# Second layer's gate and up projections: the two input halves side by side in one 512-column matmul

## The chip, the cores and the metric

One core of one Trainium2 chip runs the whole kernel. The metric is the device time of one execution in microseconds (us); the figure before is the median of three runs.

## The reference, cut to what matters

The model is one conformer-style block on 256 latent positions, followed by two layers of a diffusion-transformer block (D = 1024) on 256 latent and 256 context positions. The second of these layers needs no context output, so behind its attention it works on the 256 latent positions alone. Its feed-forward part is

```python
def swiglu(h, w_gate_up, w_down):
    gu = h @ w_gate_up
    g, u = jnp.split(gu, 2, axis=-1)
    return (jax.nn.silu(g) * u) @ w_down
```

with `w_gate_up` of 1024 x 5632 (gate and up, 2816 features each) and `w_down` of 2816 x 1024, all in float32.

## The kernel before, in words

**Precision.** TensorE multiplies in the type float32r, which keeps fewer bits than float32. So every weight W and every input x is held as a high part (the value rounded to float32r: `wh`, `xh`) and a low part (what is left: `wl`, `xl`), and a product is the sum of three matmuls, high by high, high weights by low input, and low weights by high input (`three`, lines 857 to 861). All three have 128 x 128 weights and a moving operand of 256 columns (one latent sequence, SEQ) or of 512 (latent and context, NT); in the second layer's feed-forward part it is 256.

**The weight stream.** All weights pass through SBUF in units of 128 x 1024 values (512 KB). There are four slots. For each unit SyncE loads `raw` (line 367) once GpSimd has made the low part of the unit four before it; ScalarE makes `wh` as a converting copy (line 548), once the unit has landed and TensorE is done with the unit four before it; GpSimd makes `wl = raw - wh` (line 475) and so releases the unit to TensorE. Each engine does its work in the order in which it is written, with semaphores between the engines.

**Gate and up of the second layer (phase `gu1`).** It has 22 steps. A step takes two units and gives one pair of output tiles, gate and up, of 128 features x 256 positions each: 2 outputs x 8 k-tiles x 3 matmuls = 48. I call the steps pairs 0 to 21. Steps alternate between two sets of PSUM banks (`j` = 0 and 1); before the change both tiles of a pair lie in one bank. When TensorE has finished a pair (`pair_done`), this happens: ScalarE applies Silu to the gate tile (line 699, into `sil`), VectorE multiplies it with the up tile (line 1358, `ft`), ScalarE makes its high part (line 702, `fh`), VectorE the low part (line 1361, `fl`).

**The order that matters.** In ScalarE's program (`gate_up` in the ScalarE block, lines 692 to 704), the body for pair p first converts the two units of pair p+1 (`high_step`), then waits for pair p, then does Silu and `fh`. So the units of pair p+2 are converted only behind `fh` of pair p, though their slots came free when TensorE finished pair p. GpSimd's two low parts for pair p+2 follow, and TensorE (`features`, from line 863) waits on each unit's low part before it starts it.

**Behind it** come the down projection `dn1` (12 steps of 48 matmuls, but each third one of 36, lines as above with `fh`, `fl` as input; ScalarE does nothing there but `high_step`) and a final norm and store.

Of the kernel before, what the change touches and what calls it, by code (L numbers as in the profile page):

```python
# [8 lines left out]
F32R = mybir.dt.float32r  # L9
BF16 = mybir.dt.bfloat16  # L10
ALU = mybir.AluOpType
ACT = mybir.ActivationFunctionType
AX_X = mybir.AxisListType.X

P = 128
D = 1024
KT = D // P
SEQ = 256
NT = 2 * SEQ
FF = 2816  # L20
FT = FF // P
# [38 lines left out]
PH, STEPS = plan()  # L60
# [19 lines left out]
XL_COUNT = {"m0": 6 * KT, "f0": 8 * KT, "m1": 10 * KT, "f1": 11 * KT}  # L80
# [18 lines left out]
ADA_SLOTS = 4  # L99
# [38 lines left out]
def build(nc, wall, wada, cond, xin, pin, par, tab, tab_ret, tab_rope, tab_mask, rpb, out):  # L138
    with ExitStack() as ctx:
        sems = {}  # L140

        def S(name):
            if name not in sems:
                sems[name] = ctx.enter_context(nc.semaphore(name))
            return sems[name]
# [8 lines left out]
        def at(name, shape, offset, dt=F32):  # L154
            size = 4 * int(np.prod(shape[1:]))
            assert offset + size <= base + arena_bytes, (name, offset + size - base - arena_bytes)
            return nc.alloc_sbuf_tensor_at(name, shape, dt, offset=offset)

        def sb(name, shape, dt=F32):
            o = cursor[0]  # L160
            cursor[0] = (o + 4 * int(np.prod(shape[1:])) + 31) // 32 * 32
            return at(name, shape, o, dt)
# [13 lines left out]

        h = sb("h", [P, KT, NT])
        xs_at = cursor[0]
        xh = sb("xh", [P, KT, NT], F32R)
        xl = sb("xl", [P, KT, NT], F32R)  # L180
        y = sb("y", [P, KT, NT])
        y_at = cursor[0] - 4 * KT * NT
        raw = sb("raw", [P, SLOTS, HALF, 256])
        wh = sb("wh", [P, SLOTS, HALF, 256], F32R)
        wl = sb("wl", [P, SLOTS, HALF, 256], F32R)
# [17 lines left out]
              NT: at("fl2", [P, FT, NT], big_at + 4 * FT * NT, F32R)}  # L203
        sil = at("sil", [P, 2, NT], y_at)
        ft = at("ft", [P, 2, NT], y_at + 8 * NT)


        r = Region(big_at, BIG)
# [50 lines left out]
        ps = ctx.enter_context(nc.psum_tensor("ps", [P, 8, 512], F32))  # L259
# [5 lines left out]
        ada_used = S("ada_used")  # L265
        bank_free = S("bank_free")
# [9 lines left out]
        def tile_bank(j, o, n, wide=False):  # L276

            return ps[:, j, o * SEQ:o * SEQ + SEQ] if n == SEQ and not wide else ps[:, 2 * j + o, 0:n]
# [25 lines left out]
        def pair_done(eng, ph, i, pair):  # L304

            eng.wait_ge(units_done, i * (2 * ph.body) + (2 * ph.step0 + 2 * ph.per_pair * (pair + 1) + SLOTS))
# [236 lines left out]
        def _(act):  # L543
# [145 lines left out]
            norm("fpre1", h, SEQ, 0)  # L689
            split("xr_ready", KT, y, SEQ, par_ap("ffn_pre"))  # L690

            def gate_up(ph, n, f0):

                def body(i):
                    for j in range(2):
                        high_step(ph, i, j)
                        pair_done(act, ph, i, j)
                        act.wait_ge(S("f_lo"), i * 2 + (f0 + j + 1))
                        nc.scalar.activation(sil[:, j, 0:n], tile_bank(j, 0, n), ACT.Silu).then_inc(S("silu_ready"), 1)  # L699
                        act.wait_ge(bank_free, i * 2 + (ph.pair0 + j + 3))  # L700
                        settled(act)
                        nc.scalar.activation(fh[n][:, i * 2 + j, :], ft[:, j, 0:n], ACT.Copy).then_inc(S("f_hi"), 1)  # L702
                preload(ACT.Silu)
                run(act, ph, body)
# [27 lines left out]
            for l in range(2):  # L732
# [102 lines left out]
                n = NT if l == 0 else SEQ  # L835
# [2 lines left out]
                split_shifted((3 + 2 * l) * KT, l, 3, n)  # L838
                if l == 0:
                    condition_to(csb_late)  # L840
                gate_up(PH[f"gu{l}"], n, FT * (l + 1))
                stream_only(PH[f"dn{l}"], peel=l)
            root("final", SEQ)

# [2 lines left out]
        def _(pe):  # L847
# [9 lines left out]
            def three(o, wa, wb, xa, xb, start, stop):  # L857

                nc.tensor.matmul(o, wa, xa, start=start, stop=False, skip_group_check=True)  # L859
                nc.tensor.matmul(o, wa, xb, start=False, stop=False, skip_group_check=True)  # L860
                return nc.tensor.matmul(o, wb, xa, start=False, stop=stop, skip_group_check=True)  # L861

            def features(ph, n, a=xh, b=xl, ktiles=KT, fresh=None, wide=False):


                def body(i):
                    for j in range(ph.body):
                        pair = j // ph.per_pair
                        if j % ph.per_pair == 0:
                            banks_ready(ph, i, pair)  # L870
                        for half in range(2):
                            slot = unit_ready(ph, i, j, half)
                            k0 = 2 * HALF * (j % ph.per_pair) + HALF * half
                            for o in range(2):
                                c = slice(o * P, o * P + P)
                                for kk in range(min(HALF, ktiles - k0)):
                                    k = k0 + kk
                                    if fresh and o == 0 and pair == 0:
                                        sem, n0, each = fresh
                                        pe.wait_ge(S(sem), n0 + each * (k + 1))  # L880
                                    mm = three(tile_bank(pair, o, n, wide), wh[:, slot, kk, c], wl[:, slot, kk, c],
                                               a[:, k, 0:n], b[:, k, 0:n], k == 0 and (n == NT or wide or o == 0), k == ktiles - 1)
                            mm.then_inc(units_done, 1)
                run(pe, ph, body)
# [53 lines left out]
            for hd in range(RET_H):  # L938
                b = hd % 2
# [13 lines left out]
            for hd in range(RET_H):  # L953
                pe.wait_ge(S("ret_s"), hd + 1)
                c = slice(hd * P, hd * P + P)
# [38 lines left out]
            for l in range(2):  # L994
# [158 lines left out]
                    pe.wait_ge(S("nol_ready"), 4)  # L1153
                features(PH[f"wo{l}"], n)
                norm_sum(f"f{l}", n)
                features(PH[f"gu{l}"], n, fresh=("xl_ready", XL_COUNT[f"f{l}"] - n // SEQ * KT, n // SEQ))
                features(PH[f"dn{l}"], n, fh[n], fl[n], FT, fresh=("f_lo", 2 + FT * (l + 1), 1))
            norm_sum("final", SEQ)

# [2 lines left out]
        def _(dve):  # L1162
            link = Link(dve, "dve_link")
            V = nc.vector

            for name, n in (("ada_used", ADA_SLOTS), ("bank_free", 2), ("f_lo", 2), ("osq_done", 2), ("npt_ready", 2), ("no_taken", 2)):
                dve.sem_inc(S(name), n)
            V.memset(up[:, :, 0:CONV_W - 1], 0.0)

# [56 lines left out]
            def condition(ph, i, j):  # L1226


                if ph.name not in ADA_WOVEN:
                    return  # L1230
                per, slots, a0, _ = ADA_WOVEN[ph.name]
                late = ph.name in ("gu0", "dn0")
                dve.wait_ge(S("cond_psum"), 6 if late else 2 if ph.name == "in_u" else 4)
                both = csb_late if late else csb_ps
                for s in range(per * j, per * j + per):
                    dve.wait_ge(ada_landed[s % slots],
                                i * (16 * 2 * per // slots) + 16 * (slot_tenants(ph.name, s % slots) + s // slots + 1))
                    at_ = bass.ds(i * (2 * per) + (a0 + s), 1)
                    dve.wait_ge(ada_used, i * (2 * per) + (a0 + s + ADA_SLOTS))
                    junk = unread[:].rearrange("p (a b) -> p a b", a=2)  # L1240
                    unit = ada_slot(ph.name, s % slots).rearrange("p (a b) -> p a b", a=2)
                    V.scalar_tensor_tensor(junk, unit, 1.0, both[0], ALU.mult, ALU.mult,  # L1242
                                           accum_out=mod_flat[:, at_, 0]).then_inc(S("ada_half"), 1)
                    dve.wait_ge(S("ada_half"), i * (2 * per) + (a0 + s + 1))
                    ins = V.scalar_tensor_tensor(junk, unit, 1.0, both[1], ALU.mult, ALU.mult,  # L1245
                                                 accum_out=mod_flat[:, at_, 1])
                    ins.then_inc(ada_used, 1)
# [101 lines left out]
                clear_sums(norm, n)  # L1349
                run(dve, ph, body)  # L1350

            def gate_up(ph, n, f0):
                def body(i):
                    for j in range(2):
                        condition(ph, i, j)
                        dve.wait_ge(S("f_lo"), i * 2 + (f0 + j + 1))
                        dve.wait_ge(S("silu_ready"), i * 2 + (f0 + j + 1))
                        V.tensor_tensor(ft[:, j, 0:n], sil[:, j, 0:n], tile_bank(j, 1, n), ALU.mult).then_inc(bank_free, 1)  # L1358
                        dve.wait_ge(S("f_hi"), i * 2 + (f0 + j + 1))
                        f1 = bass.ds(i * 2 + j, 1)  # L1360
                        V.tensor_tensor(fl[n][:, f1, :].rearrange("p a b -> p (a b)"), ft[:, j, 0:n],  # L1361
                                        fh[n][:, f1, :].rearrange("p a b -> p (a b)").bitcast(F32),
                                        ALU.subtract).then_inc(S("f_lo"), 1)
                run(dve, ph, body)
# [102 lines left out]
            for l in range(2):  # L1467
# [139 lines left out]
                take_gated(PH[f"wo{l}"], n, l, 0, f"f{l}")  # L1607
                recip(f"f{l}", n)
                modulate(l, 1, n)
                gate_up(PH[f"gu{l}"], n, FT * (l + 1))  # L1610
                if l == 0:
                    modulation(0, (5,))
                take_gated(PH[f"dn{l}"], n, l, 1, ("m1", "final")[l])
# [114 lines left out]
```

## Time and profile before

| | us |
|---|---|
| Median of 3 runs (1537.3 to 1539.34) | 1538.76 |
| The profiled execution's own time | 1542.9 |
| Its span, first to last instruction | 1540.8 |
| TensorE matmul busy | 1392.1 (90%) |
| GpSimd busy | 806.3 (52%) |
| VectorE busy | 819.4 (53%) |
| ScalarE busy | 590.9 (38%) |
| Gate and up of the second layer | about 1334 to 1464 of the span |
| Down of the second layer | about 1464 to 1528 |

The mean granted clock of TensorE is 0.947 of full speed. The profile is of one execution; its busy shares are averages over stages with different limits, and a matmul's busy time is longer than the distance between two matmuls, since they are pipelined. So the working below goes by start times in this stage.

### The profile page before, as it was taken

The page shows a single profiled execution, that of the slowest core. Times are in us where ns is not written, and L with a number is a line of the kernel's source. Part 1 is how long each engine was busy: PE and PEld are TensorE (multiplying, and loading weights), DVE is VectorE, ACT ScalarE, POOL GpSimd, SP SyncE. Part 2 cuts the span into 40 slices and gives each one's busy share as a digit, 9 for nine tenths or more (in the row PEclk, how much of TensorE's full clock was granted, in tenths as well). Part 3 has the DMA queues.
Part 4 walks back from the last instruction along what each step waited for, and adds up shares of the span by engine and source line. Part 5 has one row for each costly group of instructions (what it writes and reads, how often), then busy time and mean ns, then how long its engine had stood idle before and what let it go on. Part 6 is the DMA issues. An engine that isn't in the chain of part 4 may idle for free.

```text
span 1540.8 us, 25514 instructions
## 1 busy us (share of the span) xinstructions
PE 1392.1 (90%) x8734; PEld 1234.1 (80%) x8734; DVE 819.4 (53%) x1380; ACT 590.9 (38%) x938; POOL 806.3 (52%) x370
## 2 busy tenths in 40 slices
PE   5977899997789999696999999999699898799996
PEld 5976799996667878474788888888499877799996
DVE  5887755688843544736555556353504263711144
ACT  6434544444333434523332323222321264444442
POOL 3775488894535453140434444544174122588894
PEclk8998899998899999897999999999799998899998
DMA  7643377784322222010655554534094101355562
GB/s 278 228 131 137 123 273 274 277 308 144 116 67 71 83 69 83 14 55 28 224 184 191 190 215 169 203 137 177 25 258 116 41 2 54 109 179 179 187 205 95
DMA packets 82163, 227.16 MB, mean 147 GB/s; under 512 B 23872, under 2 KB 29248, under 8 KB 81856
## 3 DMA queue, kind: packets, MB, share of 16 engines
q1 hardware_dynamic: 81664, 224.91, 43.3%
q10 hardware_dynamic: 448, 1.57, 0.5%
q8 instruction: 31, 0.51, 0.1%
q14 instruction: 20, 0.16, 0.0%
HBM read 222.26 MB, written 1.05 MB: 145 GB/s over the span
## 4 chain that ended last, share of the span: by engine, by line
PE 43%; issue 33%; POOL 15%; DVE 6%; ACT 1%; DMA 1%; SPq 1%; POOLq 0%; DVEq 0%; ACTq 0%
POOL wl L475 14%; PE ps L859 11%; PE ps L860 11%; PE ps L861 11%; PE ps L902 1%; PE ps L901 1%; PE ps L900 1%; PE ps L1123 1%; PE ps L1137 1%; PE ps L1049 1%; PE ps L1075 1%; DVE rstd L1182 1%; PE ps L1115 1%; SPq L375 1%; DVE sq L1300 1%
## 5 line engine op out<-in xcount | busy, mean ns | idle before, releaser
L475 POOL TENSOR_TENSOR wl<-raw,wh 128x1024 fp32r<-128x1024 f32 x310 | 751.5, 2444 | 642.6 <-ACT wh L548 642.1
L859 PE MATMUL ps<-xh,wh 128*128 128x256 f32 (+1 forms) x1728 | 569.6, 330 | 53.5 <-DVE xl L1219 27.2
L860 PE MATMUL ps<-xl,wh 128*128 128x256 f32 (+1 forms) x1728 | 562.2, 325 | 0.0
L861 PE MATMUL ps<-xh,wl 128*128 128x256 f32 (+1 forms) x1728 | 561.8, 325 | 0.0
L548 ACT ACTIVATE wh<-raw 128x1024 fp32r<-128x1024 f32 x310 | 319.4, 1054 | 329.1 <-PE ps L861 211.1
L859 PEld LDWEIGHTS ps<-xh,wh 128*128 128x128 f32 x1728 | 336.2, 195 | 97.4 <-issue 55.5
L861 PEld LDWEIGHTS ps<-xh,wl 128*128 128x128 f32 x1728 | 336.7, 195 | 24.8
L860 PEld LDWEIGHTS ps<-xl,wh 128*128 128x128 f32 x1728 | 336.9, 195 | 23.2
L861 PE MATMUL ps<-fh,wl 128*128 128x256 f32 (+1 forms) x528 | 169.7, 321 | 0.0
L860 PE MATMUL ps<-fl,wh 128*128 128x256 f32 (+1 forms) x528 | 169.0, 320 | 0.0
L859 PE MATMUL ps<-fh,wh 128*128 128x256 f32 (+1 forms) x528 | 167.7, 318 | 0.0
L1358 DVE TENSOR_TENSOR ft<-sil,ps 128x256 f32<-128x256 f32 (+1 forms) x66 | 33.7, 510 | 193.1 <-ACT sil L699 193.1
L699 ACT ACTIVATE sil<-ps 128x256 f32<-128x256 f32 (+1 forms) x66 | 30.1, 456 | 222.9 <-PE ps L861 222.9
L859 PEld LDWEIGHTS ps<-fh,wh 128*128 128x128 f32 x528 | 100.0, 189 | 7.8
L860 PEld LDWEIGHTS ps<-fl,wh 128*128 128x128 f32 x528 | 98.9, 187 | 8.7
L861 PEld LDWEIGHTS ps<-fh,wl 128*128 128x128 f32 x528 | 99.1, 188 | 7.6
L1346 DVE SCALAR_TENSOR_TENSOR h<-ps,mod,h 128x256 f32 x48 | 20.3, 478 | 140.2 <-PE ps L861 140.0
L1242 DVE SCALAR_TENSOR_TENSOR unread<-ada_late,ps 128x1024 bf16<-128x1024 f32 x56 | 68.2, 1218 | 13.1 <-DMA ada_late<-wada 9.1
L1245 DVE SCALAR_TENSOR_TENSOR unread<-ada_late,ps 128x1024 bf16<-128x1024 f32 x56 | 68.4, 1221 | 8.2 <-DVE unread L1242 2.4
L1361 DVE TENSOR_TENSOR fl<-ft,fh 128x256 f32 (+1 forms) x66 | 36.2, 548 | 51.9 <-ACT fh L702 51.9
L756 ACT ACTIVATE e<-ps,sm 128x512 f32<-128x512 f32 (+1 forms) x64 | 36.4, 577 | 56.0 <-DVE sm L1493 39.9
L1242 DVE SCALAR_TENSOR_TENSOR unread<-ada,ps 128x1024 bf16<-128x1024 f32 x40 | 48.8, 1220 | 7.9 <-issue 3.9
(188 smaller groups left out, 1639.9 us busy)
## 6 DMA issues: line engine op xcount, KB each, us to landing
raw<-wall SPq DMA_DIRECT2D x310, 512.0 KB, 3.9
ada_late<-wada SPq DMA_DIRECT2D x56, 512.0 KB, 3.3
ada<-wada SPq DMA_DIRECT2D x40, 512.0 KB, 3.5
bias<-rpb SPq DMA_DIRECT2D x16, 256.0 KB, 7.7
h<-xin SPq DMA_DIRECT2D x2, 1024.0 KB, 7.1
sww<-qk SPq DMA_DIRECT2D x32, 64.0 KB, 2.0
csb<-cond SPq DMA_DIRECT2D x1, 1024.0 KB, 8.1
sw<-u ACTq DMA_DIRECT2D x2, 512.0 KB, 6.7
```

Source lines behind the costliest of these rows:

```text
L475: nc.gpsimd.tensor_tensor(wl[:, slot, :, :], raw[:, slot, :, :], wh[:, slot, :, :].bitcast(F32), ALU.subtract).then_inc(lo_ready, 1)
L548: nc.scalar.activation(wh[:, slot, :, :], raw[:, slot, :, :], ACT.Copy).then_inc(hi_ready, 1)
L699: nc.scalar.activation(sil[:, j, 0:n], tile_bank(j, 0, n), ACT.Silu).then_inc(S("silu_ready"), 1)
L756: nc.scalar.activation(e2[:, q, m, c], ps[:, b + m, c], ACT.Exp, scale=0.125, bias=sm[:, r6, 2 * t + m:2 * t + m + 1], accum_out=sm[:, r6, ...
L859: nc.tensor.matmul(o, wa, xa, start=start, stop=False, skip_group_check=True)
L860: nc.tensor.matmul(o, wa, xb, start=False, stop=False, skip_group_check=True)
L861: return nc.tensor.matmul(o, wb, xa, start=False, stop=stop, skip_group_check=True)
L1242: V.scalar_tensor_tensor(junk, unit, 1.0, both[0], ALU.mult, ALU.mult, accum_out=mod_flat[:, at_, 0]).then_inc(S("ada_half"), 1)
L1245: ins = V.scalar_tensor_tensor(junk, unit, 1.0, both[1], ALU.mult, ALU.mult, accum_out=mod_flat[:, at_, 1])
L1346: ins = V.scalar_tensor_tensor(hk, tile_bank(j, o, n)[:, t], g, hk, ALU.mult, ALU.add)
L1358: V.tensor_tensor(ft[:, j, 0:n], sil[:, j, 0:n], tile_bank(j, 1, n), ALU.mult).then_inc(bank_free, 1)
L1361: V.tensor_tensor(fl[n][:, f1, :].rearrange("p a b -> p (a b)"), ft[:, j, 0:n], fh[n][:, f1, :].rearrange("p a b -> p (a b)").bitcast(F32) ...
```

## The change

The high and the low input become two halves of one tensor `xhl` (same place, same order as before). In the second layer's gate and up, and there alone, the two matmuls that use the high weights become one with the moving operand `[high input | low input]`, 512 columns, into a whole PSUM bank; the third (low weights by high input) stays and adds to the bank's first half. Each pair so uses two banks in place of one. The second half of each bank must then be added to the first: ScalarE copies both second halves (128 x 512 values) to SBUF (`half_b`), VectorE adds them onto both first halves in PSUM, and Silu waits for that. In `features`, `joined` is used when `join` is given; `tile_bank(..., wide)` names the first half of the separate banks.

```diff
-        xh = sb("xh", [P, KT, NT], F32R)
-        xl = sb("xl", [P, KT, NT], F32R)
+        xhl = sb("xhl", [P, 2, KT, NT], F32R)
+        xh, xl = xhl[:, 0, :, :], xhl[:, 1, :, :]
...
+        half_b = at("half_b", [P, 2, SEQ], y_at + 16 * NT)
...
-            def gate_up(ph, n, f0):
+            def gate_up(ph, n, f0, join=False):
                 def body(i):
                     for j in range(2):
                         high_step(ph, i, j)
                         pair_done(act, ph, i, j)
+                        if join:
+                            act.wait_ge(S("halves_added"), i * 2 + (j + 1))
+                            nc.scalar.activation(half_b[:], ps[:, 2 * j:2 * j + 2, SEQ:NT], ACT.Copy).then_inc(S("half_copied"), 1)
+                            act.wait_ge(S("halves_added"), i * 2 + (j + 2))
                         act.wait_ge(S("f_lo"), i * 2 + (f0 + j + 1))
-                        nc.scalar.activation(sil[:, j, 0:n], tile_bank(j, 0, n), ACT.Silu).then_inc(S("silu_ready"), 1)
+                        nc.scalar.activation(sil[:, j, 0:n], tile_bank(j, 0, n, join), ACT.Silu).then_inc(S("silu_ready"), 1)
...
+            def joined(o, wa, wb, x, k, last):
+
+                nc.tensor.matmul(o, wa, x[:, :, k, 0:SEQ], start=k == 0, stop=False, skip_group_check=True)
+                return nc.tensor.matmul(o[:, 0:SEQ], wb, x[:, 0, k, 0:SEQ], start=False, stop=k == last, skip_group_check=True)
...
+                                    if join is not None:
+                                        mm = joined(ps[:, 2 * pair + o, :], wh[:, slot, kk, c], wl[:, slot, kk, c], join, k, ktiles - 1)
+                                        continue
...
-                features(PH[f"gu{l}"], n, fresh=("xl_ready", XL_COUNT[f"f{l}"] - n // SEQ * KT, n // SEQ))
+                features(PH[f"gu{l}"], n, fresh=("xl_ready", XL_COUNT[f"f{l}"] - n // SEQ * KT, n // SEQ),
+                         join=xhl if l else None)
...
-            def gate_up(ph, n, f0):
+            def gate_up(ph, n, f0, join=False):
                 def body(i):
                     for j in range(2):
                         condition(ph, i, j)
+                        if join:
+                            dve.wait_ge(S("half_copied"), i * 2 + (j + 1))
+                            two = ps[:, 2 * j:2 * j + 2, 0:SEQ]
+                            V.tensor_tensor(two, two, half_b[:], ALU.add).then_inc(S("halves_added"), 1)
...
-                        V.tensor_tensor(ft[:, j, 0:n], sil[:, j, 0:n], tile_bank(j, 1, n), ALU.mult).then_inc(bank_free, 1)
+                        V.tensor_tensor(ft[:, j, 0:n], sil[:, j, 0:n], tile_bank(j, 1, n, join), ALU.mult).then_inc(bank_free, 1)
```

## Rows read from the trace of the kernel before

**Rows 1.** The page's first part: busy time of each engine, share, instructions.
```profile
PE 1392.1 (90%) x8734; PEld 1234.1 (80%) x8734; DVE 819.4 (53%) x1380; ACT 590.9 (38%) x938; POOL 806.3 (52%) x370
```

**Rows 2.** Busy time by stretch: PE, PEld, DVE, ACT, POOL, clock, DMA share, GB/s.
```profile
1349.00:1464.00 115.00, 115.00 (x961) 115.00 (x960) 16.93 (x40) 55.07 (x80) 94.67 (x41) 1.00 0.55 183
...
1470.00:1520.00 50.00, 50.00 (x419) 50.00 (x419) 23.33 (x15) 21.49 (x21) 49.39 (x21) 1.00 0.57 189
```

**Rows 3.** Waits from 1344 to 1530: total us, times, longest.
```profile
POOL wl L475 <- ACT wh L548: 21.8, 22, 1.5
```

**Rows 4.** Timeline (start, us, instruction) of PE in the stage: 256 columns.
```profile
1383.06 0.28 PE L859 MATMUL ps<-xh,wh 128*128 128x256 f32 x1
1383.18 0.28 PE L860 MATMUL ps<-xl,wh 128*128 128x256 f32 x1
```

**Rows 5.** Timeline of PE in the first layer's gate and up: 512 columns.
```profile
899.79 0.39 PE L859 MATMUL ps<-xh,wh 128*128 128x512 f32 x1
...
903.87 0.39 PE L859 MATMUL ps<-xh,wh 128*128 128x512 f32 x1
```

**Rows 6.** Timeline of ACT over one pair of the stage.
```profile
1372.18 0.39 ACT L699 ACTIVATE sil<-ps 128x256 f32<-128x256 f32 x1 [2.40 <-PE ps L861]
1373.23 0.42 ACT L702 ACTIVATE fh<-ft 128x256 f32 x1 [0.67 <-DVE ft L1358]
1373.64 2.01 ACT L548 ACTIVATE wh<-raw 128x1024 fp32r<-128x1024 f32 x2
1377.95 0.38 ACT L699 ACTIVATE sil<-ps 128x256 f32<-128x256 f32 x1 [2.30 <-PE ps L861]
```

**Rows 7.** Timeline of DVE at the same pair.
```profile
1372.67 0.42 DVE L1358 TENSOR_TENSOR ft<-sil,ps 128x256 f32<-128x256 f32 x1 [4.20 <-ACT sil L699]
```

**Rows 8.** Timeline of POOL at this pair and the next.
```profile
1374.78 4.76 POOL L475 TENSOR_TENSOR wl<-raw,wh 128x1024 fp32r<-128x1024 f32 x2 [1.10 <-ACT wh L548]
1380.43 4.77 POOL L475 TENSOR_TENSOR wl<-raw,wh 128x1024 fp32r<-128x1024 f32 x2 [0.89 <-ACT wh L548]
```

**Rows 9.** Timeline of pairs 0 and 1, where PE once waits for POOL.
```profile
1340.56 4.76 POOL L475 TENSOR_TENSOR wl<-raw,wh 128x1024 fp32r<-128x1024 f32 x2 [16.87 <-ACT wh L548]
...
1341.91 0.28 PE L861 MATMUL ps<-xh,wl 128*128 128x256 f32 x1
1342.30 0.38 ACT L699 ACTIVATE sil<-ps 128x256 f32<-128x256 f32 x1 [0.87 <-PE ps L861]
...
1343.00 0.39 PE L859 MATMUL ps<-xh,wh 128*128 128x256 f32 x1 [0.81 <-POOL wl L475]
...
1348.86 0.28 PE L859 MATMUL ps<-xh,wh 128*128 128x256 f32 x1
...
1349.14 0.38 ACT L699 ACTIVATE sil<-ps 128x256 f32<-128x256 f32 x1 [3.48 <-PE ps L861]
```

**Rows 10.** Groups by line and shape: count, busy us, mean ns, idle before.
```profile
L767 ACT ACTIVATE pt<-ps 128x512 f32<-128x512 f32 x24 | 14.4, 598 | 41.3 <-PE ps L1064 41.3
...
L1580 DVE TENSOR_TENSOR ps<-ps,bias 128x512 f32<-128x512 f32 x16 | 11.2, 699 | 11.2 <-PE ps L1137 11.2
...
L1358 DVE TENSOR_TENSOR ft<-sil,ps 128x512 f32<-128x512 f32 x22 | 15.1, 688 | 69.4 <-ACT sil L699 69.4
```

**Rows 11.** Timeline: DVE operations that run beside POOL's low parts.
```profile
745.60 4.75 POOL L475 TENSOR_TENSOR wl<-raw,wh 128x1024 fp32r<-128x1024 f32 x2 [5.99 <-ACT wh L548]
...
749.81 0.69 DVE L1358 TENSOR_TENSOR ft<-sil,ps 128x512 f32<-128x512 f32 x1 [4.39 <-ACT sil L699]
...
1343.92 1.69 DVE L1361 TENSOR_TENSOR fl<-ft,fh 128x256 f32 x1 [0.71 <-ACT fh L702]
```

**Rows 12.** Busy time of PE alone in the attention stage: PE, clock, DMA, GB/s.
```profile
1285.00:1290.00 5.00, 3.91 (x34) 1.00 0.00 0
```

**Rows 13.** Timelines of ACT and POOL at the end of the stage (pair 21).
```profile
1464.34 0.38 ACT L699 ACTIVATE sil<-ps 128x256 f32<-128x256 f32 x1 [2.40 <-PE ps L861]
...
1466.84 44.21 POOL L475 TENSOR_TENSOR wl<-raw,wh 128x1024 fp32r<-128x1024 f32 x18 [1.01 <-ACT wh L548]
```

More of the change, by code:

```diff
@@ L840, in _ @@
                     condition_to(csb_late)
-                gate_up(PH[f"gu{l}"], n, FT * (l + 1))
+                gate_up(PH[f"gu{l}"], n, FT * (l + 1), l == 1)
                 stream_only(PH[f"dn{l}"], peel=l)
@@ L861, in three, with features @@
                 return nc.tensor.matmul(o, wb, xa, start=False, stop=stop, skip_group_check=True)
-            def features(ph, n, a=xh, b=xl, ktiles=KT, fresh=None, wide=False):
+            def joined(o, wa, wb, x, k, last):
+                nc.tensor.matmul(o, wa, x[:, :, k, 0:SEQ], start=k == 0, stop=False, skip_group_check=True)
+                return nc.tensor.matmul(o[:, 0:SEQ], wb, x[:, 0, k, 0:SEQ], start=False, stop=k == last, skip_group_check=True)
+            def features(ph, n, a=xh, b=xl, ktiles=KT, fresh=None, wide=False, join=None):
                 def body(i):
@@ L1164, in _ @@
             V = nc.vector
-            for name, n in (("ada_used", ADA_SLOTS), ("bank_free", 2), ("f_lo", 2), ("osq_done", 2), ("npt_ready", 2), ("no_taken", 2)):
+            for name, n in (("ada_used", ADA_SLOTS), ("bank_free", 2), ("f_lo", 2), ("osq_done", 2), ("npt_ready", 2), ("no_taken", 2), ("halves_added", 1)):
                 dve.sem_inc(S(name), n)
@@ L1609, in _ @@
                 modulate(l, 1, n)
-                gate_up(PH[f"gu{l}"], n, FT * (l + 1))
+                gate_up(PH[f"gu{l}"], n, FT * (l + 1), l == 1)
                 if l == 0:
```

## The prediction

> **What bounds the kernel now.** I began with the page: TensorE is busy 90% of the span, with one weight load for each matmul [rows 1]. That is an average, so I went to the stretches. From 1349 to 1464, gate and up of the second layer, TensorE is busy all the time at the full granted clock (1.00, the 2.4 GHz level), while GpSimd is busy 94.67 of 115 us; in the down projection behind it TensorE is full again, and GpSimd nearly so [rows 2]. The waits say the same: TensorE waits for nobody in this stage, and GpSimd waits 22 times for ScalarE, about 1 us each [rows 3]. So today the stage goes by the distance of matmuls, 0.12 us for 256 columns [rows 4], 48 x 0.12 = 5.76 us a pair. A shorter pair on TensorE would shorten the span one for one, as long as the next low part is there in time. How near that second limit is, the timelines of ScalarE, VectorE and GpSimd at one pair tell.
>
> **The second limit.** Take pair p, whose Silu starts at 1372.18 [rows 6]. VectorE's product starts at 1372.67 [rows 7], `fh` at 1373.23, and then ScalarE converts the two units of pair p+2, from 1373.64 [rows 6]. GpSimd starts on them at 1374.78, 2.60 us behind the start of Silu; for the other set of banks it is 1380.43 - 1377.95 = 2.48 [rows 6, 8]. One low part is 4.76 / 2 = 2.38, say 2.39. So the first low part of pair p+2 is done at 1377.17. TensorE wants it one pair behind pair p. Silu follows pair p's last matmul by 0.39 (1341.91 to 1342.30) [rows 9], and the next matmul would follow it by 0.12; so pair p+1 started at about 1372.18 - 0.39 + 0.12 = 1371.91, and p+2 starts at 1377.67. **The slack is 0.5 us**, or 0.6 in the other parity. The reader is to see that the chain runs over two pairs: end of pair p, Silu, product, `fh`, conversion, low part, pair p+2.
>
> One place shows TensorE at that limit: GpSimd's first low part of pair 1 ends at 1340.56 + 2.38 = 1342.94, and TensorE starts the pair at 1343.00, 0.06 later, after a wait of 0.81; Silu of that pair comes at 1349.14, and pair 2 would start at 1348.86, which is 5.86 after the start, so a stalled start costs 0.10 more than a flowing one [rows 9].
>
> **What the change removes.** 22 pairs x 2 outputs x 8 k-tiles = 352 matmuls and as many weight loads go. The columns stay: 768 per k-tile. 512 columns take (903.87 - 899.79) / 18 = 0.227 us [rows 5], where two of 256 take 0.240 [rows 4]; 0.0133 x 352 = 4.7 us. A pair becomes 16 x (0.227 + 0.120) = 5.55 us, 0.21 less. By the Trainium skill (TensorE: Matmul & The Clock Gate, Back-to-back issue gap) an isolated warm matmul needs N / 2.4 + 2.5 ns, which as an estimate would make a removed matmul worth 2.5 ns, 0.9 us for all 352. The rows differ, with 13.3 ns over the columns' time, and the rows decide.
>
> The moving operand now consists of two runs of 256 columns in two places. No row shows such a one. It can hardly be faster than one run; slower by at most what splitting it costs today, 0.0133 a matmul, 0.21 a pair. I take nothing, as the 512-column rows are the nearest, and keep 0.21 for the range.
>
> **What it adds**, for each pair, all of it ahead of Silu, and so in the chain of two pairs:
> - ScalarE's copy of 128 x 512 out of PSUM: 0.60 (line 767, 24 of them, mean 598 ns) [rows 10].
> - ScalarE to VectorE: Silu ends at 1372.57, the product starts at 1372.67: 0.10 [rows 6, 7].
> - VectorE's add of 128 x 512 in place in PSUM: 0.70. Line 1580 is the same form, two half banks and an SBUF operand, mean 699 ns [rows 10].
> - VectorE to ScalarE: the product ends at 1373.09, `fh` starts at 1373.23: 0.14 [rows 6, 7].
>
> Together X = 1.54 us. It can't be below 0.60 + 0.69 = 1.29, the two operations alone; above, three more register-addressed waits a pair could each show a little: I allow 0.3 and take 1.54.
>
> The price of the add needs a look, since GpSimd is at work beside it. `fl` of pair 0 (both inputs in SBUF) took 1.69 in place of 0.42 while a low part ran; the product with one input in PSUM took 0.69, undisturbed, beside low parts that run from 745.60 to 750.35 [rows 11]. The add has one input in each, so it goes by the second. The Trainium skill (SBUF — State Buffer, SBUF: two separate sides) says that a VectorE operation with two SBUF inputs and a GpSimd operation that reads SBUF exclude each other; by that rule, the trace agrees, 1.69 against 0.69.
>
> What waits behind the new wait: on ScalarE the Silu, `fh` and both conversions for pair p+2; then GpSimd, TensorE, and SyncE's loads, which go by GpSimd's low parts. Banks, `sil` and `half_b` are free in time: the product frees the banks under 3 us behind the pair's end, and they are wanted 5.5 us behind it. The weights' loads have time too: a slot is reloaded from the end of its low part and converted some 8.9 us later. The new first waits of copy (`halves_added`) are met already. Moving `xh` and `xl` into one tensor changes no address and costs nothing.
>
> **The sum.** From a stalled start of an odd pair to the start two pairs later: 0.10 + 5.55 of TensorE, less one distance of 0.12 and plus 0.39 to the copy: 5.92; X 1.54; Silu to GpSimd 2.60; low part 2.39; release 0.06. **12.51 us for two pairs**, against 11.52 now and 11.10 if TensorE set the pace. For the even pairs it is 12.39. So the slower, odd chain sets it: from pair 1 (1343.00, whose start hangs on a conversion that ScalarE does at 1339.44, ahead of anything new) over pairs 3, 5, ... 21 to the second step of the down projection, whose units are converted behind pair 21's `fh` just the same: 11 double steps, 137.6 us, to 1480.6. Today that step starts 21 x 5.76 = 120.96 after pair 2's 1348.86, at 1469.8. **The change costs 10.8 us**; the removed 4.7 are in it.
>
> Behind that the down projection stays as it is. TensorE takes 2.88 a unit, GpSimd 44.21 / 18 = 2.46 [rows 13], so GpSimd runs ahead again; only each sixth unit takes TensorE 1.44, where its lead shrinks to some 0.3. I take nothing, and keep 1 us for the range. Silu of the last pair should come at 1343.00 + 10 x 12.51 + 5.92 + 1.54 = 1475.6 in place of 1464.34 [rows 13].
>
> The profiled execution took 1542.9, 4.1 above the median of 1538.76. 1542.9 + 10.8 = 1553.7 for such a one; the median should be 1538.8 + 10.8 = 1549.6, or 0.7% more.
>
> **The rivals.**
> - *Faster: TensorE still sets the pace.* The place is the wait for the low part of pair p+2. If the chain's slack covered X, the whole 4.7 us would come: 1534.0. Without X and without a stalled start the odd chain takes 12.51 - 1.54 - 0.10 = 10.87 us, against 11.10 of TensorE; so X must stay under 11.10 - 10.87 = 0.23 for the full gain, and under 11.52 - 10.97 = 0.55 for any. The copy alone is 0.60. For it speaks that TensorE never waits today; against it all of rows 6 to 10. Chance 0.03.
> - *No change within 0.2%*: X from about 0.3 to 0.8 (0.55, and 3.1 / 11 = 0.28 to either side), if copy and add overlapped or the two handshakes vanished. They can't overlap, each waits for the other. Chance 0.03.
> - *The clock.* A TensorE that stalls each second pair by 1 us could be granted 1.2 GHz at times. Where it was busy for 3.91 of 5 us it kept 1.00 [rows 12], and here it would be busy 89%. Were one pair in ten at the lower level, that is two pairs, 11 us more: 1561. Chance 0.03.
> - *The add is held up by GpSimd* as `fl` was: X grows by about 1.0 in most pairs, 11 us more: 1561. Chance 0.04, since the rows of 11 speak against it.
> - *The new operand is slow* (0.21 a pair, once per double step, 2.3 us) and the waits show (0.3 x 11 = 3.3 us): that is still the forecast's case, up to 1556.
>
> **How the numbers follow.** The chain as reckoned has 0.87. Its own range: X from 1.29 to 1.84 is -2.8 to +3.3 us, the operand up to +2.3, the down projection up to +1, not all at once; with the even chain setting the pace 1.3 less. That gives 1545 to 1556, and as the other cases hold 0.13 the range stays there. A difference of about 0.2%, 3 us, is what a measurement of this kernel can tell from none. Faster 0.03, same 0.03, slower 0.94.
>
> **What would show it.** In the changed trace TensorE waits for GpSimd's `wl` in the stage, about 1.0 us ahead of odd pairs and 0.3 or less ahead of even ones, where there was no wait; GpSimd's idle time before it, put down to ScalarE's `wh`, grows from 1 to about 1.5 us a pair; Silu starts come 12.5 us apart over two pairs; copy 0.60, add 0.70, copy to Silu 1.54; distances of 0.227 and 0.12 on TensorE; clock 1.00. Pairs of 5.55 without waits would prove me wrong, and so would an add of over 1 us or a copy-to-Silu distance under 0.6.

## The result and the profile after

The changed kernel takes 1546.65 us (median of 7 runs, 1543.08 to 1551.38), the kernel before 1537.3 (7 runs, 1534.23 to 1541.2): ratio 1.0061, interval 1.004 to 1.0081. It is slower by some 9 us, where 10.8 were forecast.

The page of the changed kernel, where span and TensorE's row answer to [rows 1]:

```profile
span 1541.3 us, 24921 instructions
PE 1388.5 (90%) x8382; PEld 1210.8 (79%) x8382; DVE 844.8 (55%) x1402; ACT 604.4 (39%) x960; POOL 805.7 (52%) x370
```

The span is only 0.5 us above that of before, and that misleads. This profiled execution took 1543.08, the lowest of its seven, and that of before 1542.9, above all seven of its own; the stages ahead of the change ran 8.4 us shorter in it (the stage's first matmul starts at 1325.64 in place of 1334.06). They are the same work in both. So I compare **from the stage's first matmul to the end of the span**: 1540.8 - 1334.06 = 206.7 us before, 1541.3 - 1325.64 = 215.7 after, 8.9 more. The experiments are read with the same two points.

Timelines of the changed kernel at pairs 1 to 3, merged from TensorE, ScalarE, VectorE and GpSimd (start us, us, instruction); they answer to [rows 6 to 9]:

```profile
1334.59 0.49 PE L870 MATMUL ps<-xhl,wh 128*128 128x512 f32 x1 [0.75 <-POOL wl L476]
1334.93 0.28 PE L871 MATMUL ps<-xhl,wl 128*128 128x256 f32 x1
...
1340.13 0.28 PE L871 MATMUL ps<-xhl,wl 128*128 128x256 f32 x1
1340.45 0.60 ACT L701 ACTIVATE half_b<-ps 128x512 f32<-128x512 f32 x1 [1.69 <-PE ps L871]
1341.08 0.70 DVE L1373 TENSOR_TENSOR ps<-ps,half_b 128x512 f32<-128x512 f32 x1 [3.63 <-ACT half_b L701]
1341.89 0.38 ACT L704 ACTIVATE sil<-ps 128x256 f32<-128x256 f32 x1 [0.84 <-DVE ps L1373]
1342.37 0.42 DVE L1376 TENSOR_TENSOR ft<-sil,ps 128x256 f32<-128x256 f32 x1 [0.60 <-ACT sil L704]
1342.92 0.42 ACT L707 ACTIVATE fh<-ft 128x256 f32 x1 [0.65 <-DVE ft L1376]
1343.34 2.01 ACT L549 ACTIVATE wh<-raw 128x1024 fp32r<-128x1024 f32 x2
1344.47 4.74 POOL L476 TENSOR_TENSOR wl<-raw,wh 128x1024 fp32r<-128x1024 f32 x2 [1.82 <-ACT wh L549]
...
1345.89 0.27 PE L871 MATMUL ps<-xhl,wl 128*128 128x256 f32 x1
1346.91 0.50 PE L870 MATMUL ps<-xhl,wh 128*128 128x512 f32 x1 [0.75 <-POOL wl L476]
1347.26 0.28 PE L871 MATMUL ps<-xhl,wl 128*128 128x256 f32 x1
...
1352.55 0.28 PE L871 MATMUL ps<-xhl,wl 128*128 128x256 f32 x1
```

The reader is to follow one turn of the chain. Pair 1 starts at 1334.59; its end reaches ScalarE at 1340.45; copy, add and their handshakes put Silu at 1341.89; the conversions for pair 3 come at 1343.34, GpSimd at 1344.47, and pair 3 starts at 1346.91, where TensorE, done with pair 2, would have started at about 1346.0. 12.32 us for two pairs. TensorE waits like this ahead of every odd pair and ahead of the second step of the down projection, 12 times in all: 0.53 to 0.93 us each by the waits' rows, the first of them (0.75) being the one that before had too. Ahead of even pairs the rows list none; the most that the starts show is 0.13, at pair 6. The last two lines, of pair 3, are for the experiments on the matmuls.

The waits of the changed kernel from 1330 to 1535, total us, times, longest; the first row answers to [rows 3]:

```profile
POOL wl L476 <- ACT wh L549: 48.5, 24, 16.9
...
PE ps L870 <- POOL wl L476: 9.0, 11, 0.9
```

Less the one wait of 16.9 ahead of the stage, GpSimd now waits 31.6 us for ScalarE, 23 times, 1.4 each. A stretch of the stage, with [rows 2] for comparison (columns as there):

```profile
1349.00:1460.00 111.00, 103.51 (x575) 87.41 (x574) 27.82 (x54) 60.07 (x90) 85.08 (x37) 1.00 0.50 168
```

TensorE, busy throughout before, is busy 93% now, at the full granted clock, and GpSimd 77%: neither is the bound. The bound is the chain through all four engines.

### The profile page after: what moved, and what is told of

Read it like the earlier page. It is cut to its first block, busy times and chain, and to the rows that moved or that the text cites. A ratio compares the mean times of both kernels' runs of the same rounds, so it can differ in the third digit from the quotient of the medians.

```text
span 1541.3 us, 24921 instructions
## 1 busy us (share of the span) xinstructions
PE 1388.5 (90%) x8382; PEld 1210.8 (79%) x8382; DVE 844.8 (55%) x1402; ACT 604.4 (39%) x960; POOL 805.7 (52%) x370
## 4 chain that ended last, share of the span: by engine, by line
PE 60%; issue 19%; POOL 12%; DVE 5%; SPq 1%; ACT 1%; DMA 0%; POOLq 0%; DVEq 0%; ACTq 0%
PE ps L864 17%; PE ps L866 16%; PE ps L865 16%; POOL wl L476 11%; PE ps L915 1%; PE ps L914 1%; PE ps L913 1%; PE ps L1136 1%; PE ps L1088 1%; PE ps L1062 1%; PE ps L1150 1%; DVE rstd L1196 1%; PE ps L1128 1%; DVE y L1225 1%; SPq L376 1%
## 5 line engine op out<-in xcount | busy, mean ns | idle before, releaser
L864 PE MATMUL ps<-xhl,wh 128*128 128x256 f32 (+1 forms) x1376 | 466.6, 339 | 49.0 <-DVE xhl L1233 23.0
L865 PE MATMUL ps<-xhl,wh 128*128 128x256 f32 (+1 forms) x1376 | 459.8, 334 | 0.0
L866 PE MATMUL ps<-xhl,wl 128*128 128x256 f32 (+1 forms) x1376 | 459.7, 334 | 0.0
L864 PEld LDWEIGHTS ps<-xhl,wh 128*128 128x128 f32 x1376 | 266.3, 194 | 91.6 <-issue 48.0
L866 PEld LDWEIGHTS ps<-xhl,wl 128*128 128x128 f32 x1376 | 266.8, 194 | 24.5
L865 PEld LDWEIGHTS ps<-xhl,wh 128*128 128x128 f32 x1376 | 267.1, 194 | 22.9
L870 PE MATMUL ps<-xhl,wh 128*128 128x512 f32 x352 | 127.9, 406 | 13.1 <-POOL wl L476 9.0
L871 PE MATMUL ps<-xhl,wl 128*128 128x256 f32 x352 | 99.1, 281 | 0.0
L870 PEld LDWEIGHTS ps<-xhl,wh 128*128 128x128 f32 x352 | 66.8, 190 | 34.3 <-POOL wl L476 13.7
```

The source lines that it names most:

```text
L870: nc.tensor.matmul(o, wa, x[:, :, k, 0:SEQ], start=k == 0, stop=False, skip_group_check=True)
L871: return nc.tensor.matmul(o[:, 0:SEQ], wb, x[:, 0, k, 0:SEQ], start=False, stop=k == last, skip_group_check=True)
```

## The experiments

The theory: copy and add stand ahead of the conversions in ScalarE's order, and so in the chain over two pairs. The rivals: the joined matmuls are themselves slow; or the copy and the add cost by being there, wherever they stand. Times from the stage's first matmul to the first of the down projection (stage) and to the end of the span (to end), from one profile each; ratios of whole executions to the kernel before, with 95% intervals. Both sides of a ratio ran on one chip, but the experiments used four chips in all (rows 3 to 5 of the table one, 6 to 8 another, 9 and 10 a third, the last a fourth). Whole executions spread by about 8 us, so a difference of 2 us between versions is read from the stage.

| version | stage | to end | ratio |
|---|---|---|---|
| before | 130.0 | 206.7 | |
| changed | 138.3 | 215.7 | 1.0061 (1.004 to 1.0081) |
| joined, no copy and add | 127.8 | 203.9 | 0.9978 (0.9962 to 0.9993) |
| copy and add, not joined | 140.7 | 217.7 | 1.0074 (1.0057 to 1.0091) |
| copy twice | 144.5 | 221.8 | 1.0093 (1.007 to 1.0117) |
| convert first | 127.8 | 204.5 | 0.9973 (0.9956 to 0.9991) |
| convert between | 127.8 | 204.0 | 0.9972 (0.9957 to 0.9987) |
| before, convert first | 130.0 | 206.2 | 0.9998 (0.9981 to 1.0016) |
| convert first, operand in one run | 127.8 | 204.0 | 0.9978 (0.9965 to 0.9992) |
| changed, operand in one run | 139.2 | 215.8 | 1.0063 (1.0039 to 1.0088) |
| convert between, grouped | 126.9 | 203.1 | 0.9965 (0.9944 to 0.9986) |

**Joined matmuls without copy and add.** High weights by low input are left out of gate and up.

```diff
-                            act.wait_ge(S("halves_added"), i * 2 + (j + 1))
-                            nc.scalar.activation(half_b[:], ps[:, 2 * j:2 * j + 2, SEQ:NT], ACT.Copy).then_inc(S("half_copied"), 1)
-                            act.wait_ge(S("halves_added"), i * 2 + (j + 2))
...
-                            V.tensor_tensor(two, two, half_b[:], ALU.add).then_inc(S("halves_added"), 1)
```

> The 512-column matmul stays; copy and add of the halves are taken out (the product of high weights and low input is left out of gate and up). Measured from the stage's first matmul to the end of the span, the kernel before has 1540.8 - 1334.06 = 206.7 us, the changed one 1541.3 - 1325.64 = 215.7. Theory (the chain over two pairs): without the 1.44 us of copy, add and handshakes the chain takes 12.32 - 1.44 - 0.10 = 10.8 us for two pairs, less than TensorE's 11.10; no wait of TensorE between pairs 2 and 21, 21 pairs shortened by 0.21, 202.3 us, the whole 4.4 us faster than before. Rival (TensorE itself pays for the operand in two places or for the second bank): it stays near 215 us. Rival (half and half): between.

The loss is gone. TensorE's one wait for GpSimd in the stage is the old one ahead of pair 1:

```profile
PE ps L866 <- POOL wl L476: 0.7, 1, 0.7
```

But the stage gained 2.2 us, not 4.4: (127.76 - 8.93) / 21 = 5.66 us a pair, where 5.55 was reckoned and 5.76 stood. In this version the joined matmul pays by half of what I gave it.

**Copy and add without joined matmuls.** The matmuls are the old three, in the new banks:

```diff
-                                        mm = joined(ps[:, 2 * pair + o, :], wh[:, slot, kk, c], wl[:, slot, kk, c], join, k, ktiles - 1)
+                                        mm = three(ps[:, 2 * pair + o, 0:SEQ], wh[:, slot, kk, c], wl[:, slot, kk, c],
+                                                   a[:, k, 0:n], b[:, k, 0:n], k == 0, k == ktiles - 1)
...
-                            nc.scalar.activation(half_b[:], ps[:, 2 * j:2 * j + 2, SEQ:NT], ACT.Copy).then_inc(S("half_copied"), 1)
+                            nc.scalar.activation(half_b[:], ps[:, 2 * j:2 * j + 2, SEQ:NT], ACT.Copy, scale=0.0).then_inc(S("half_copied"), 1)
```

> The three 256-column matmuls of before, in the banks of the changed kernel, with copy and add kept (the copy multiplies by zero, so that nothing is added). Theory: 12.32 + 0.21 = 12.53 us for two pairs against 11.52, 11 times: 206.7 + 11.1 = 217.8 us. Rival (the cost lies in the 512-column matmuls): 207.

217.7: the whole loss comes with copy and add alone, and the joined matmul takes 2 us off it. This version also measures the slack. Two pairs take (140.65 - 8.96) / 10.5 = 12.54 us, 1.02 more than the 11.52 of before, though 1.44 of copy, add and handshakes and 0.10 of a stalled start were put in: 0.52 was absorbed, where the prediction had 0.5.

**The copy twice.**

```diff
+                            nc.scalar.activation(half_c[:], ps[:, 2 * j:2 * j + 2, SEQ:NT], ACT.Copy)
                             nc.scalar.activation(half_b[:], ps[:, 2 * j:2 * j + 2, SEQ:NT], ACT.Copy).then_inc(S("half_copied"), 1)
```

> The changed kernel with ScalarE's copy made twice, once into a buffer that nobody reads. Theory: each 1 us put into the chain costs 11 us, so 0.50 to 0.60 more per pair gives 215.7 + 6 = 221 to 222 us, and waits of TensorE ahead of odd pairs grow by 0.5 to 0.6. Rival (the add of VectorE beside GpSimd, or something else that ScalarE's time does not move): 216.

221.8, 6.1 more, or 0.55 for each of eleven double steps; the second copy starts 0.50 behind the first (1385.33 and 1385.83). The cost came as expected. The waits did not: those ahead of odd pairs did not grow by 0.5 to 0.6, but TensorE now waits 20 times, ahead of each pair from the second on, and longer ahead of the even ones (1.04 at pair 2, 0.54 at the least) than ahead of the odd ones (0.16 at pair 3, up to 0.55). The total rose from 9.0:

```profile
PE ps L872 <- POOL wl L477: 11.3, 20, 1.0
```

The chain fixes how long two pairs take together, not which of the two waits. In this execution TensorE's granted clock was still 0.50, the 1.2 GHz level, from 1336 to 1338, and pair 0's last matmul started 8.7 us behind the stage's first one, against 7.9 in the profile of the changed kernel (1333.57 - 1325.64). The even pairs hang on that end. The same holds for the version with copy and add alone and for that with the old order and the operand in one run: the last matmul of pair 0 at 8.7, the longer waits ahead of the even pairs at first.

**The order turned round**: in this stage ScalarE converts for pair p+2 directly behind the end of pair p; the down projection's conversions move up by one step with it.

```diff
-                        high_step(ph, i, j)
+                        if not join:
+                            high_step(ph, i, j)
                         pair_done(act, ph, i, j)
+                        if join:
+                            high_step(ph, i, j + 1)
                         if join:
                             act.wait_ge(S("halves_added"), i * 2 + (j + 1))
...
                 preload(ACT.Silu)
+                if join:
+                    high_step(ph, 0, 0)
                 run(act, ph, body)
...
                     for j in range(ph.body):
-                        high_step(ph, i, j)
+                        high_step(ph, i, j + ahead)
```

> The changed kernel with ScalarE's order turned round in this stage: behind the end of pair p it first converts the two units of pair p+2, then copies the halves, then Silu and the high part. The same operations in number. Theory (the order puts the copy and the add into the chain): the low part of pair p+2 is ready about 3.7 us after the end of pair p, TensorE waits for nothing from pair 2 on, 202.3 us from the stage's first matmul to the end of the span, 4.4 us less than the kernel before, about 1533 against 1537.3. The banks are free about 4.5 us after the end of the pair, in time. Rival (the extra operations cost by being there, through load or ports): it stays at 215.

**The same with the conversions between**: copy, one conversion, Silu, the other, high part (`high_step` takes the half as an argument).

```diff
                             nc.scalar.activation(half_b[:], ps[:, 2 * j:2 * j + 2, SEQ:NT], ACT.Copy).then_inc(S("half_copied"), 1)
+                            high_step(ph, i, j + 1, (0,))
                             act.wait_ge(S("halves_added"), i * 2 + (j + 2))
...
+                        if join:
+                            high_step(ph, i, j + 1, (1,))
                         act.wait_ge(bank_free, i * 2 + (ph.pair0 + j + 3))
```

> As the one before, but the copy first, then one conversion in the shadow of VectorE's add, Silu, the other conversion in the shadow of the product, the high part. Theory: 202.3 us too; the low part is ready about 4.3 us after the end of the pair. Rival: 215.

Both are below the kernel before, with the copy and the add still there; that excludes the rival of their mere presence. ScalarE over one pair of the second of them:

```profile
1383.88 0.60 ACT L702 ACTIVATE half_b<-ps 128x512 f32<-128x512 f32 x1 [2.65 <-PE ps L877]
1384.38 1.06 ACT L549 ACTIVATE wh<-raw 128x1024 fp32r<-128x1024 f32 x1
1385.33 0.38 ACT L706 ACTIVATE sil<-ps 128x256 f32<-128x256 f32 x1
1385.61 1.05 ACT L549 ACTIVATE wh<-raw 128x1024 fp32r<-128x1024 f32 x1
1386.56 0.40 ACT L711 ACTIVATE fh<-ft 128x256 f32 x1
1389.46 0.60 ACT L702 ACTIVATE half_b<-ps 128x512 f32<-128x512 f32 x1 [2.50 <-PE ps L877]
```

No bracket of idle time stands within the pair: each conversion fills a time in which ScalarE would have waited for VectorE. These two pairs come 5.58 apart, 5.66 on average, TensorE's own pace; again the stage gives 2.2 and not 4.4. The ratios of the two versions stand for some 4 us, but with intervals from 1.4 to 6.8 us: they do not tell 2.2 from 4.4, and the stage does.

**The kernel before, conversions ahead of Silu**, with no joined matmul:

> The kernel before, with the conversions ahead of Silu and no joined matmuls. Theory: TensorE already set the pace, so nothing is gained: 206.7 us, ratio 1.000. Rival (the order alone would have brought what the version with both brings): 202.

Ratio 0.9998, stage 130.0: the order alone brings nothing, since nothing but TensorE bound that stage. The gain needs both, the joined matmul and the order that takes its copy and add out of the chain.

**Why a pair takes 5.66.** In these versions a joined k-tile takes 0.3537 (5.66 / 16), 0.007 more than 0.227 + 0.120. My first idea was the operand's two places, the bound that I had kept. The low input of this stage goes to the unused context columns of the high input's tensor, so that one run of 512 columns is read:

```diff
-                nc.tensor.matmul(o, wa, x[:, :, k, 0:SEQ], start=k == 0, stop=False, skip_group_check=True)
+                nc.tensor.matmul(o, wa, x[:, k, :], start=k == 0, stop=False, skip_group_check=True)
...
-                        V.scalar_tensor_tensor(xl[:, k, t], y[:, k, t], mod[:, l, section(l, 3 * w) + k, c:c + 1],
+                        to = xh[:, k, SEQ:NT] if (l, w) == (1, 1) else xl[:, k, t]
+                        V.scalar_tensor_tensor(to, y[:, k, t], mod[:, l, section(l, 3 * w) + k, c:c + 1],
```

> The version that converts first, and the low input of this stage written into the unused context columns of the high input's tensor, so that the 512 moving columns are one run in place of two 256-column runs 16 KB apart. In the version that converts first, a k-tile took 0.2335 to 0.239 + 0.120 to 0.115 = 0.3535 us, where 0.227 + 0.120 = 0.347 were reckoned; its stage took 127.8 us from the first matmul to the first of the down projection, and 204.5 to the end of the span. Theory (the second run costs about 7 ns a matmul): 0.227 + 0.120, 5.55 us a pair, stage 127.8 - 22 x 16 x 0.0067 = 125.4, to the end 202.2. Rival (it is the change between 512 and 256 columns, or between banks, that costs): unchanged, 0.3535 and 127.8.

> The changed kernel, order untouched, with the one-run operand alone. Theory of the chain: a pair's time on TensorE stands once in each two pairs, so only 11 x 16 x 0.0067 = 1.2 us come of it at most: 214.5 to 215.7 us from the first matmul to the end of the span, waits of TensorE as before or longer, still slower than the kernel before by 8 to 9 us. Rival (the slow operand was the cause of the loss): near 204.

The idea fell: 127.8 as before it, 5.66 a pair. With the old order it changes nothing either (215.8), and shows once more that the loss is not the operand's. Next, four matmuls of 512 columns in a row, then four of 256:

```diff
-                                        mm = joined(ps[:, 2 * pair + o, :], wh[:, slot, kk, c], wl[:, slot, kk, c], join, k, ktiles - 1)
+                                        nc.tensor.matmul(ps[:, 2 * pair + o, :], wh[:, slot, kk, c], join[:, :, k, 0:SEQ],
+                                                         start=k == 0, stop=False, skip_group_check=True)
...
+                                for kk in range(HALF if join is not None else 0):
+                                    k = k0 + kk
+                                    mm = nc.tensor.matmul(ps[:, 2 * pair + o, 0:SEQ], wl[:, slot, kk, c], join[:, 0, k, 0:SEQ],
+                                                          start=False, stop=k == ktiles - 1, skip_group_check=True)
```

> The version that converts between, with the matmuls of each half step grouped: four of 512 columns one behind the other, then four of 256, in place of 512 and 256 by turns. The same matmuls and weight loads in number. There a pair took (127.76 - 8.93) / 21 = 5.659 us, 0.3537 a k-tile, and the operand as one run changed nothing. Theory A (the turn from one length to the other costs): a pair nears 16 x 0.3467 = 5.55 plus a quarter of the 0.11, 5.57, and the stage takes 8.93 + 21 x 5.57 = 126.0 from the first matmul to the first of the down projection. Theory B (each matmul behind a weight load of its own carries it, whatever stands beside it): 5.66 and 127.8 again.

It fell between the two: stage 126.9, (126.92 - 8.95) / 21 = 5.62 a pair. TensorE's timeline of this version:

```profile
1387.39 1.09 PE L898 MATMUL ps<-xhl,wh 128*128 128x512 f32 x4
1388.32 0.64 PE L905 MATMUL ps<-xhl,wl 128*128 128x256 f32 x4
1388.79 1.09 PE L898 MATMUL ps<-xhl,wh 128*128 128x512 f32 x4
```

Four of 512 take 0.93 from start to start, 0.2325 each, and four of 256 take 0.47. Grouping won 0.04 of the missing 0.11 us a pair; why 512 columns take 0.2325 here and 0.227 in the first layer's stage [rows 5] stays open. This version has the lowest ratio of all, 0.9965, though its interval overlaps those of the other two.

The trace of the changed kernel narrows it. There the joined k-tile has two lengths, by pairs. From the second k-tile to the last, pair 1 takes (1340.13 - 1334.93) / 15 = 0.347 us a k-tile, just what was reckoned, and pair 3 (1352.55 - 1347.26) / 15 = 0.353. Of the 21 pairs behind pair 0, 13 run at 0.347 and 8 at 0.353; in the versions in which TensorE does not wait between pairs (no copy and add, convert first, convert between), all 21 run at 0.353. So neither the joined operand nor the turn from 512 to 256 columns costs time by itself. What decides between the two lengths is not shown.

## Why the prediction was right, point by point

- **The bound before** (TensorE, with a second limit 0.5 us behind): shown. Without copy and add the joined kernel is faster; with them alone it is slower by 11, which leaves a slack of 0.52.
- **X**, forecast 1.54: measured 1340.45 to 1341.89, 1.44, and the same in all 22 pairs within 0.01. The copy (0.60, all 22 within 2 ns) and the add (0.70) came as the rows of their forms had them; the handshake from copy to add was 0.03 and not 0.10, that from add to Silu 0.11 and not 0.14. The add ran undisturbed beside GpSimd, 698 to 700 ns in all 22, so that rival is out.
- **The double step**, forecast 12.51: 5.86 (5.92) of TensorE, 1.44 (1.54), 2.58 (2.60) to GpSimd, 2.44 (2.45) of low part and release, together 12.32. The 5.86 is 5.54 from the stalled start to the last matmul, forecast 5.53, and 0.32 from there to the copy (1340.13 to 1340.45), where pair 0 of the kernel before had shown 0.39. Over all eleven it is (144.88 - 8.95) / 11 = 12.36: five take 12.40 to 12.42, just those whose odd pair runs at 0.353 a k-tile, five 12.32 or 12.33, and the last 12.23. The second step of the down projection starts 144.9 after the stage's first matmul, 135.8 before: 9.1 more, where 10.8 were forecast. The missing 1.7 is 11 x 0.15: 0.10 of it X, 0.07 the start of the copy.
- **What the change removes**, forecast 4.7 us: the term that was mis-sized most. Where TensorE sets the pace it measured 2.2, since all pairs then run at 0.3537 a k-tile and not at 0.347. In the changed kernel 13 of 21 pairs did run at 0.347, and under the chain a pair's time counts once in two pairs, so five slow odd pairs cost the forecast 0.5 us. But the rival in which TensorE keeps the pace would have brought 2.2 us and not 4.7.
- **The waits**: ahead of odd pairs as forecast, 0.7 to 0.9 by the rows where about 1.0 was said; ahead of even pairs 0.13 at most, where 0.3 or less was said. That they stood ahead of the odd pairs is in part luck: with the old order and the operand in one run, where pair 0 ended 0.8 us later, the longer waits stood ahead of the even pairs at first, at the same cost (215.8 against 215.7). **The down projection** took 77.3 us from its first matmul to the end, against 76.7: its first step is 0.80 longer (6.56 against 5.76) by the stall ahead of the second, and the rest differs by 0.2. **The clock** was 1.00 from pair 1 on.
- Against the run-to-run spread of about 8 us in the rest of the kernel, the ratio of 1.0061 fits 1.007.

## What to carry to other kernels

Before adding work behind a matmul group, find what the engine that does it has queued behind it, and follow that to the next group's start: here 1.4 us a pair, on engines that were busy less than half of this stage before (ScalarE 55 of 115 us, VectorE 17), cost 9 us, because the weights' conversion stood behind it. If the chain has less slack than the addition, move the feeding work ahead of it, or into its handshakes; the same operations then left a gain of 2.2 us in the stage instead. And read a local change between two points of the same stage: two spans alone would have said here that nothing had changed.

## What was not expected of the hardware

Where TensorE never waited, a 512-column matmul by turns with a 256-column one took 0.354 us for both in every pair, and grouped by four 0.351, against 0.227 + 0.120 from the stages that have but one length. In the changed kernel, where it waits ahead of each second pair, both together took 0.347 in 13 of 21 pairs and 0.353 in 8, with the same instructions and at the same granted clock of 1.00. Whether the moving columns lie in one run or in two 16 KB apart made no difference (127.8 us for the stage in both).
